# A two-block transformer layer on one core: angle tables split and moved, delta steps regrouped, memory attention read from PSUM

## The reference, cut to what matters

```
# block 1: hybrid mixer, then a convolutional FFN
x = layer_norm(x); mod = silu(c) @ w_ada + b_ada          # shift, scale, gate rows
h = x * (1 + scale) + shift
proj = h @ w_in;  q, k, v = silu(causal_conv(...))        # 4 heads of 128
# gated delta rule in chunks: (I + L) sol = rhs, L strictly lower; S carried from chunk to chunk
o = gated_delta_rule(l2_norm(q), l2_norm(k), v, log_a, beta); o = rms_norm(o) * silu(z)
# ... gated linear attention, w_o, FFN
# block 2
q, k = rope(q, positions), rope(k, positions)             # angles = position * inv_freq
# ... dilated window attention, RG-LRU, w_out
s = (xn @ wq) (memn @ wk)^T * 128 ** -0.5                 # 4 heads, 256 memory rows
o = (softmax(s) @ (memn @ wv)) @ wo
# ... MLP, final rms norm
```

## Time and profile before

| | |
|---|---|
| median of 3 runs | 3453.81 us |
| profiled execution, its own time | 3454.77 us |
| its span, first to last instruction | 3453.5 us |
| busy: PE, PE weight load | 3146.9 us (91%), 2146.5 us (62%) |
| busy: DVE, ACT, POOL | 1465.2 us (42%), 1037.6 us (30%), 750.3 us (22%) |
| mean granted TensorE clock | 0.954 |
| moved by DMA | 189.33 MB, mean 55 GB/s |

### The profile page before, as it was taken

One profiled execution on the slowest core, in us unless ns is written; L12 is line 12 of the kernel. 1 busy time (PEld: TensorE's weight loads), 2 busy tenths in 40 slices (PEclk: granted clock), 3 DMA queues, 4 the chain that ended last, 5 costly groups with the idle time before them and its releaser, 6 DMA issues.

```text
span 3453.5 us, 32104 instructions
## 1 busy us (share of the span) xinstructions
PE 3146.9 (91%) x12812; PEld 2146.5 (62%) x12812; DVE 1465.2 (42%) x2378; ACT 1037.6 (30%) x1699; POOL 750.3 (22%) x448
## 2 busy tenths in 40 slices
PE   2999978788997999999997999999977799999997
PEld 1445556566544888888875444585433488888886
DVE  4335533323254554555546443572222233333334
ACT  1225533333312222222224540263333422221123
POOL 0300012111024444444442111100000322222221
PEclk7999999999998999999998999999988799999998
DMA  6211101110323111111113012002201111111111
GB/s 206 82 31 31 31 19 55 55 56 19 110 97 98 62 49 49 46 47 49 49 44 91 25 45 61 19 3 69 85 25 49 37 55 49 49 49 47 47 48 55
DMA packets 199586, 189.33 MB, mean 55 GB/s; under 512 B 16183, under 2 KB 147663, under 8 KB 199439
## 3 DMA queue, kind: packets, MB, share of 16 engines
q1 hardware_dynamic: 198864, 187.09, 17.2%
q10 hardware_dynamic: 575, 0.20, 0.0%
HBM read 175.43 MB, written 9.70 MB: 54 GB/s over the span
## 4 chain that ended last, share of the span: by engine, by line
PE 85%; DVE 6%; ACT 5%; issue 3%; POOL 1%; DMA 1%; ACTq 0%; SPq 0%; DVEq 0%; POOLq 0%
PE bank L1041 62%; PE bank L1067 7%; PE bank L1136 3%; PE bank L1360 2%; PE bank L1005 1%; PE bank L1344 1%; PE bank L1193 1%; PE bank L1202 1%; PE bank L1314 1%; PE bank L1336 1%; DVE stats L1502 1%; PE bank L1403 1%; PE bank L1028 1%; PE bank L1333 1%; DVE resid L1568 1%
## 5 line engine op out<-in xcount | busy, mean ns | idle before, releaser
L1041 PE MATMUL bank<-ft,panel 128*128 128x512 f32 x832 | 360.7, 594 | 5.1 <-ACT ft L2219 4.1
L1041 PE MATMUL bank<-ft_hi,panel_hi 128*128 128x512 f32 x704 | 278.2, 395 | 14.8 <-POOL ft_lo L2620 9.3
L1041 PEld LDWEIGHTS bank<-ft,panel 128*128 128x128 f32 x832 | 158.1, 191 | 204.2 <-issue 204.2
L1067 PE MATMUL bank<-ft,panel 128*128 128x512 f32 x576 | 272.4, 612 | 9.4 <-ACT z L2304 6.2
L1041 PE MATMUL bank<-ft_hi,panel_lo 128*128 128x512 f32 x704 | 278.4, 395 | 0.0
L1041 PE MATMUL bank<-ft_lo,panel_hi 128*128 128x512 f32 x704 | 277.5, 394 | 0.0
L2564 POOL TENSOR_TENSOR panel_lo<-panel,panelm_hi 128x1024 fp32r<-128x1024 f32 x64 | 153.3, 2397 | 507.8 <-ACT panelm_hi L2175 507.8
L1891 DVE TENSOR_SCALAR ffn_conv<-ffn_in,ffn_taps 128x512 f32<-128x512 f32 x88 | 112.9, 1283 | 316.4 <-ACT ffn_in L2427 316.4
L2142 DVE TENSOR_TENSOR resid<-resid,bank 128x512 f32<-128x512 f32 x256 | 174.8, 688 | 151.3 <-PE bank L1041 150.5
L1041 PE MATMUL bank<-ftm_hi,panelm_hi 128*128 128x512 f32 x512 | 203.4, 397 | 23.1 <-issue 12.9
L2564 POOL TENSOR_TENSOR panel_lo<-panel,panel_hi 128x1024 fp32r<-128x1024 f32 x66 | 158.0, 2401 | 247.8 <-ACT panel_hi L2175 247.8
(11 more groups left out here) (439 smaller groups left out, 5612.6 us busy)
## 6 DMA issues: line engine op xcount, KB each, us to landing
panel<-in_w_in SPq DMA_DIRECT2D x52, 512.0 KB, 3.7
panel<-in_w_ada SPq DMA_DIRECT2D x48, 512.0 KB, 3.8
panel<-in_ffn_w_up SPq DMA_DIRECT2D x44, 512.0 KB, 3.7
panel<-in_w_mlp_in SPq DMA_DIRECT2D x32, 512.0 KB, 4.0
panel<-in_w_mlp_out SPq DMA_DIRECT2D x32, 512.0 KB, 3.6
panel<-in_w_o SPq DMA_DIRECT2D x24, 512.0 KB, 3.6
panel<-in_w_out SPq DMA_DIRECT2D x24, 512.0 KB, 3.6
panel<-in_ffn_w_down SPq DMA_DIRECT2D x22, 512.0 KB, 3.5
```

The lines of the kernel that those rows point to most:

```text
L1041: m = te.matmul(ps, a, b, start=(start and j == 0), stop=(stop and j == len(pairs) - 1))
L1067: m = te.matmul(ps[:], w[0][:, kk, :], k.ft[:, kk, half(h)], start=(kk == 0), stop=(kk == KD - 1))
```

## The change

**Start.** `tables` is cut into three units. `positions` (three SP loads) stands right behind `constants` and before `x_load`; `angles` (DVE only) stands before `vectors`; `masks` (DVE's masks and ACT's two Sin) stands behind `condition` and before the moments. The angle tiles are now 128 partitions of 512 positions: rows 0 to 63 hold the first half of the positions, rows 64 to 127 the second. The sign is applied to the angle before Sin, in two instructions. SP stores the mask and then four half tables, and `ln0_features` waits for all five on one semaphore.

**Delta rule.** There are 22 steps: "begin" comes after "scores"; the lag stays 11. What waits for the norms moves from "decay" to "rest"; DVE's last decay product moves to "scores"; the transpose lt, DVE's qd and inv, and ACT's copy of kt move to "begin".

**Memory attention.** The queries are evicted times -128 ** -0.5. DVE takes the minimum of the negated scores directly from PSUM, and ACT does the Exp directly from PSUM with that as bias and scale -1, so ACT's scaling and DVE's negation are gone. Scores are issued five units ahead, across the pairs too, into eight buffers; `c_finish` is two units ahead. Banks: scores 0 to 3, transposes 4 and 5, products 6 and 7.

```diff
-DELTA_STEPS = (["spread", "decay", "rest", "scores"] + [...left1, right1 ... left6, right6...] +
+DELTA_STEPS = (["spread", "decay", "rest", "scores", "begin"] + [...] +
...
     k.unit("constants")
+    k.unit("positions")
+    k.unit("x_load")
+    k.unit("angles")
...
     k.unit("condition")
-    k.unit("x_load")
+    k.unit("masks")
...
         k.unit("ln0_norm", n)
-    k.unit("tables")
...
+            later = (i, u + C_AHEAD) if u + C_AHEAD < 2 * NT else (i + 1, u + C_AHEAD - 2 * NT)
+            if later[0] < CROSS // 2:
+                c_score(*later)
+            soon = (i, u + 2) if u + 2 < 2 * NT else (i + 1, u + 2 - 2 * NT)
+            if soon[0] < CROSS // 2:
+                k.unit("c_finish", *soon)
+            k.banks.take(("c_turn", i, u), (4, 5))
             k.unit("c_turn", i, u)
             if u % 4 == 1 and u > 4:
-                c_weigh(u - 5)
-        c_weigh(2 * NT - 4)
+                c_weigh(i, u - 5)
+            elif u == 1 and i:
+                c_weigh(i - 1, 2 * NT - 4)
+    c_weigh(CROSS // 2 - 1, 2 * NT - 4)
...
@@ PE, delta @@
             turned(("delta", n, "kt"), lambda h: t.k[:, h, :])
+        elif s == "begin":
             pe.wait_ge("delta_dve", n, "ltm")
             turned(("delta", n, "lt"), lambda h: t.ltm[:, h, :])
...
@@ DVE, delta @@
             evict(dve.tensor_copy(words(t.b_row), v.bank("delta", n, "b_row")[:]), "delta", n, "b_row")
+        elif s == "rest":
             for what, src, dst, sq in (("nq", ...), ("nk", ...)):
...
             did(dve.tensor_scalar(t.decay[:], t.decay[:], 0.0, None, ALU.min), "min")
+        elif s == "scores":
             v.wait_ge("delta_act", n, "decay")
             did(dve.tensor_tensor(t.decay[:], t.decay[:], spread(k.upper[:], 1, H4), ALU.mult), "decay")
-        elif s == "scores":
...
             did(dve.tensor_tensor(t.inv_t[:], ID4, t.ltm[:], ALU.subtract), "inv_t")
+        elif s == "begin":
             v.wait_ge("delta_act", n, "g_row")
...
@@ DVE and ACT, memory attention @@
-        v.wait_ge(*v.evicted("c_score", i, u))
-        dve.tensor_reduce(st[:, 0:1], s[:], AX, ALU.max).then_inc(*v.new("c_max", i, u))
-        v.wait_ge("c_max", i, u)
-        dve.tensor_scalar(st[:, 1:2], st[:, 0:1], -1.0, None, ALU.mult).then_inc(*v.new("c_bias", i, u))
+        v.wait_ge(*v.filled("c_score", i, u))
+        dve.tensor_reduce(st[:, 0:1], v.bank("c_score", i, u)[:, 0:MEM], AX, ALU.min).then_inc(*v.new("c_least", i, u))
...
-        evict(act.mul(s[:], a.bank("c_score", i, u)[:, 0:MEM], float(P) ** -0.5), "c_score", i, u)
-        a.wait_ge("c_bias", i, u)
-        act.activation(s[:], s[:], ACT.Exp, bias=st[:, 1:2], accum_out=st[:, 2:3]).then_inc(*a.new("c_exp", i, u))
+        a.wait_ge("c_least", i, u)
+        evict(act.activation(s[:], a.bank("c_score", i, u)[:, 0:MEM], ACT.Exp, bias=st[:, 0:1], scale=-1.0,
+                             accum_out=st[:, 2:3]), "c_score", i, u)
...
@@ SP @@
-        sync.dma_start(k.pos_i[0:64, :], d["positions_2"][0].partition_broadcast(64)).then_inc(
-            *sp.new("positions_loaded", 1, step=16))
+        for h in range(HALVES):
+            sync.dma_start(k.pos_i[64 * h:64 * h + 64, :], d["positions_2"][0, half(h)].partition_broadcast(64)).then_inc(
+                *sp.new("positions_loaded", 1 + h, step=16))
```

More of the change, by code:

```diff
@@ L212, in in_turn @@
     return out
-DELTA_STEPS = (["spread", "decay", "rest", "scores"] + [f"{what}{lv}" for lv in range(1, 7) for what in ("left", "right")] +
+DELTA_STEPS = (["spread", "decay", "rest", "scores", "begin"] + [f"{what}{lv}" for lv in range(1, 7) for what in ("left", "right")] +
                ["carry", "pause", "solve", "out", "norm"])
-DELTA_BANKS = {"decay": ("g_row", "g_col", "b_row", "nq", "nk"), "scores": ("kk", "kq", "vt", "kt", "lt"),
+DELTA_BANKS = {"decay": ("g_row", "g_col", "b_row", "nq", "nk"), "scores": ("kk", "kq", "vt", "kt"),
+               "begin": ("lt",),
                "carry": ("ks",), "solve": ("vn",), "out": ("o", "st"), "norm": ("rms",)}
@@ L1542, in ln0_features @@
         v.wait_ge("modulation", 0, "done")
-        for what in ("masks", "cos", "sin"):
-            v.wait_ge("tables_stored", what)
+        v.wait_ge("tables_stored", 4)
         features(0, n, k.ft[:, 0:4, tile(n)], lambda j: k.in_scale[:, 0, j:j + 1], lambda j: k.in_bias[:, 0, j:j + 1])
@@ L1971, in rglru, with did, done, angles @@
         did(dve.tensor_tensor(y, y, k.h_f[:], ALU.mult), "out")
[L1973 to L1984 removed]
+    def did(ins, *what):
+        ins.then_inc(*v.new("tables", *what))
+    def done(*what):
+        v.wait_ge("tables", *what)
+    def angles():
+        ang, turns, pos = k.ang[:], k.turns[:], k.pos_i[:]
+        v.wait_ge("positions_loaded", 2)
         did(dve.tensor_copy(ang, pos), "pos")
         done("pos")
[L1987 removed]
+        did(dve.tensor_scalar(ang, ang, k.inv_freq[:], None, ALU.mult), "ang")
         done("ang")
@@ L1991, in tables @@
         c3 = 2 * math.pi - c1 - c2
-        for name, out, quarter in (("sin", k.sin_w[some, :], 0.0), ("cos", k.cos_w[some, :], 0.25)):
+        for name, out, quarter in (("sin", k.sin_w[:], 0.0), ("cos", k.cos_w[:], 0.25)):
             did(dve.tensor_scalar(turns, ang, 1.0 / (2 * math.pi), quarter, ALU.mult, ALU.add), name, 0)
@@ L2007, in tables, with masks @@
             did(dve.tensor_scalar(out, out, -math.pi, None, ALU.max), name, 7)
+        done("sin", 7)
+        for rows in (slice(0, 32), slice(64, 96)):
+            m = dve.tensor_scalar(k.sin_w[rows, :], k.sin_w[rows, :], -1.0, None, ALU.mult)
+        did(m, "sign")
+    def masks():
+        done("cos", 7)
         v.wait_ge("constants", "distances")
@@ L2230, in ln0_features @@
         a.wait_ge("modulation", 0, "done")
-        for what in ("masks", "cos", "sin"):
-            a.wait_ge("tables_stored", what)
+        a.wait_ge("tables_stored", 4)
         features(0, n, k.ft[:, :, tile(n)], lambda j: k.in_scale[:, 0, j:j + 1], lambda j: k.in_bias[:, 0, j:j + 1])
@@ L2279, in project @@
             a.wait_ge(*a.filled(stage, c, h))
-            evict(act.copy(k.mix2[:, c, half(h)], ps[:]), stage, c, h)
+            evict(act.mul(k.mix2[:, c, half(h)], ps[:], -float(P) ** -0.5), stage, c, h)
     def ada_out(i, n):
@@ L2472, in rglru, with masks @@
             act.activation(k.th[z][:], k.th[z][:], ACT.Sqrt).then_inc(*a.new("rglru_act", i, "root", z))
-    def tables():
-        for name, x in (("sin", k.sin_w), ("cos", k.cos_w)):
-            a.wait_ge("tables", name, 7)
-            act.activation(x[0:64, :], x[0:64, :], ACT.Sin).then_inc(*a.new("tables_act", name))
+    def masks():
+        for name, x in (("sign", k.sin_w), ("cos", k.cos_w)):
+            a.wait_ge("tables", *((name, 7) if name == "cos" else (name,)))
+            act.activation(x[:], x[:], ACT.Sin).then_inc(*a.new("tables_act", name))
     def weights(t):
```

87 lines of the change are left out of this document (38 added, 49 removed).

## The result

The changed kernel takes 3357.43 us (median of 4 runs, 3355.95 to 3359.01), beside 3454.27 us for the kernel before on the same chip (4 runs): a ratio of 0.9725, 95% interval 0.9713 to 0.9737. That is 96.8 us gained where 86 were forecast; 3357 lies in the range of 3340 to 3402 and in the forecast's own, 3352 to 3386. The profiled span is 3354.7 us, 98.8 less than before, with a mean granted clock of 0.965 instead of 0.954.

A forecast was written before the change was run, and what follows sets the result against it. The prediction took PE's idle or half-clock time as the bound (85% of the wait chain is PE). Gains of 17 (start), 25 (delta) and 44 (memory attention) sum to 86 us: 3369, median 3368; own range 3352 to 3386, 8-in-10 range 3340 to 3402.

The forecast's parts named there:

- The gap at right5: Delta stage: PE's gap goes from 6.64 to 4.5 us, released by ACT's copy of left5; 15 us over 7 chunks.
- The wait at L1142: Delta stage: lt's wait for the masked matrix, 8.8 us in 8 times, gets covered; 7 us gained.
- the long gap: Delta stage: PE's largest gap, once a chunk before left6, 34.8 us in 6 waits; counted as 7.
- The term for the clock: Delta stage: the half clock behind the gap stays but becomes a little shorter; 3 us gained in all.
- the fall of the clock, 4: Memory attention: the wait for the pipe's fill may take the clock down for some us; 4 us charged.
- the 0.42 taken: Memory attention: DVE's minimum from PSUM takes 0.42 us per unit, between 0.41 and 0.69.
- ACT's queue would hold the delta stage: Rival, delta stage: left5's copy behind Ln and Exp makes a gap as long as before; gain 0, 3393 us; chance 0.12.
- shorter gaps let the clock stay up: Rival, delta stage: shorter gaps keep PE's clock up; 24 us more gained, 3344 us; chance 0.09.
- the forecast's own rule in the rival below it: Delta stage, in the slower-than-before rival: each us at half clock loses half a us.
- The slower rival: Delta stage: two shorter gaps per chunk keep the clock down, making the kernel slower than before; 3460 us at 0.70; chance 0.02.
- Memory attention at half clock: Rival, memory attention: PE becomes its bound at 2.2 us per unit, gain 16 instead of 44, 3396 us; chance 0.10.
- late positions: Rival, start: angles run past the vectors by up to 11 us, 3379 us; within the forecast's range, no separate chance.

The follow-up runs named there:

- start_stores: Changed kernel with the five stores of masks and angles issued behind five of the modulation's products, not behind the last modulation panels; 3350.33 us, ratio 0.9702.
- delta_only: Kernel before with only the delta rule's part of the change; 3423.73 us, ratio 0.9914.
- start_late: Changed kernel with DVE's masks behind the deviation, ACT's two Sin left in place, and angle and mask stores issued earlier; 3348.25 us, ratio 0.9685.
- delta_split: Changed kernel with both norm Ln first and both Exp at the head of "rest", behind ACT's copy of left5; 3317.46 us, ratio 0.9595.
- start_only: Kernel before with only the start's part of the change; 3438.82 us, ratio 0.9956.
- memory_ops: Changed kernel with memory attention's new operations but old order of work, four buffers and the common ring of banks; 3372.45 us, ratio 0.9775.
- delta_pair: Changed kernel with ACT's four norm instructions per delta chunk ordered Ln, Ln, Exp, Exp instead of Ln, Exp, Ln, Exp; 3321.05 us, ratio 0.9613.

## Why the prediction was right, and where its sizes were off

**Start.** Right in its mechanism, 1.9 us too small. The angles cost 11.4 us (10 taken) and ran under the vectors' wait, since the positions were there by 4.8 us (their loads took 2.9, 4 taken). Masks and moments cost what was summed; the vectors came 1.4 us earlier than in the earlier trace rows. Behind the copy nothing was shortened, as forecast: 26.0 us from the first turn to `ft` before and 26.3 after, where 1 us was charged for the stores. What the forecast did not see is that the wait of `ft` for the stores, 8.5 us, could be had by itself. `start_stores` has it.

**Delta stage.** The gap at right5 was put at 4.5 us in the chunk shown and released by ACT's copy; it is 4.41 and is. The wait at L1142 was to give 7 and gave 7.2. Over the stage, the long gap with the seventh chunk's, which a filling's wait for ACT takes (34.8 and 6.2), and the waits at right5 (4.0) came to 45.0 us; the same waits now come to 28.6 (27.0 and 1.6), so 16.4 less, 15 taken. PE's idle time fell by 26.7 us (79.6 to 52.8), 22 taken; a part the prediction did not have is a wait for POOL (3.2 to 0.9). The term for the clock was wrong in sign: 3 gained were expected, and busy PE rose by 3.4. Sum 23.3 of 25: two errors of 5 and 6 us cancelled, and that the total came so close is luck.

**Memory attention.** 45.9 of 44. The first transpose comes 4.0 us after the start, as taken. The transposes then follow each other at 1.17 us in the first pair and 1.21 in the second, 1.2 taken. From the last unit's transposes to the end it is 4.4 us, where 1 was taken behind the last unit; the fall of the clock, 4, did not come: it is 1.00 in the whole stage. So here too two errors nearly cancel. DVE's minimum from PSUM takes 418 ns, its maximum from SBUF 420, so the 0.42 taken was right. The trace does not bear out the 0.49 by the formula of the Trainium skill (VectorE: DVE Perf Modes, The TRN2 errata).

**Untouched stages.** The sum had no term for them, and they gave 10.8 us; this is most of the difference between 98.8 and 86. For the 4.2 between the delta stage and memory attention: over all fourteen profiles that stretch, the same instructions in each, is 1626.9 to 1631.5 us long, with busy PE between 1559.5 and 1564.8. It was short also in `delta_only`, and long in `start_late` and `delta_split`. Gaps in it bring the clock down for a shorter or longer time. This does not follow simply from what was edited ahead: `start_only` left it as it was (1631.3), and `memory_ops`, which has the changed kernel's work and order up to memory attention, has 1630.7 instead of 1627.2, and 426.2 instead of 430.3 in the delta stage. The sum of the two stretches goes with the delta steps, as said above, so the 4.2 us belong to the delta part more than to chance. What decides how the sum is split I did not find.

**The rivals.** That ACT's queue would hold the delta stage was half true: its copy does hold right5, at the price that the forecast gave it. That shorter gaps let the clock stay up did not happen in the changed kernel, but the mechanism is there: with at most 1.8 us before right5, `delta_pair` gained 21 us of busy PE. That this is near the rival's 24 is luck. The 24 came from "some 27 of them lost" of 82 us at half clock, where the forecast's own rule in the rival below it, half a us for each, gives 41; `delta_pair` lost 48 us at half clock for its 21, and still has 33 left. The slower rival needed a mean clock below 0.71 in the stage; it stayed at 0.91. Memory attention at half clock, and late positions, did not occur.

## What to carry to other kernels

When a wait is moved rather than removed, follow the queue of the engine that releases the next one: here the residue was two pairs of Ln and Exp in a costly order on ScalarE, and it was worth 39 us in its stage and 36 in all, more than each of two of the change's three parts. Where the rows show half clock behind a PE gap, price it in two parts: the gap, and what it does to the products after it. The second part did not come back here when the longest gaps of a chunk went from 6.6 to 4.4 us, and came back in good part at 1.8; whether it will in another kernel has to be read from its clock. Read a stretch together with the one behind it before calling a few us there chance. Before moving a step, look also at what it frees: a PSUM bank can be waited for like a value.

## What the hardware showed that was not expected

- The two Sin needed no table load of their own behind the Silu: the load at 20.71 us was followed by Silu and both Sin. In the kernel before, behind an Exp, they had one of 1.28 us.
- Exp over 256 columns takes 469 ns from PSUM and 508 from SBUF, DVE's minimum from PSUM 418 and its maximum from SBUF 420: reading scores directly from PSUM cost nothing and spared ACT's scaled copy (367 ns).
- In the delta stage, waits of 5.8 us on the mean and then of at most 4.4 us left the mean clock at 0.91 (81 us at half clock in either kernel); with 1.8 us at most before right5 it is 0.96 (33 us).
